# Token rows of expert 4 issued by ScalarE, behind its gate function of expert 2, in place of SyncE

## The reference, cut to what matters

```
scores = sigmoid(x @ w_router)                  # 384 tokens, 16 experts in 4 groups
best group by the sum of its top 2; top 2 experts of that group; weights w normalised
act = silu(x @ w_gate[e]) * (x @ w_up[e])       # w_gate, w_up: 1024 x 512 per expert
y = sum over the two chosen e of w[e] * (act @ w_down[e])   # w_down: 512 x 1024
```

## Time and profile before

| | us |
|---|---|
| median of 3 runs | 1435.25 (1432.86 to 1435.38) |
| the profiled execution | 1432.73 |
| its span, first to last instruction | 1430.9 |
| TensorE busy | 1298.1 (91%) |
| VectorE busy | 496.8 (35%) |
| ScalarE busy | 318.8 (22%) |
| share of q1 (SyncE's queue) of the DMA engines' span | 61.1% |
| share of q10 (ScalarE's queue) | 4.2% |
| mean granted clock of TensorE | 0.979 |

### The profile page before, as it was taken

One profiled execution on the slowest core, in us unless ns is written; L12 is line 12 of the kernel. 1 busy time (PEld: TensorE's weight loads), 2 busy tenths in 40 slices (PEclk: granted clock), 3 DMA queues, 4 the chain that ended last, 5 costly groups with the idle time before them and its releaser, 6 DMA issues.

```text
span 1430.9 us, 17501 instructions
## 1 busy us (share of the span) xinstructions
PE 1298.1 (91%) x6833; PEld 742.8 (52%) x6834; DVE 496.8 (35%) x881; ACT 318.8 (22%) x489; POOL 259.0 (18%) x225
## 2 busy tenths in 40 slices
PE   6999999999999969889879999999999999998773
PEld 3555446675546535445536554555655554554431
DVE  2325427862145101111154353577413531110104
ACT  2136416631001100000021562464100110000001
POOL 2730017821000100000128000684200010000001
PEclk9999999999999979999989999999999999999998
DMA  9897426654437999999974231576442579999996
GB/s 348 259 344 265 177 84 230 220 192 148 176 117 296 355 380 386 387 396 391 415 255 138 69 112 59 175 242 238 163 176 118 216 278 366 367 387 386 408 416 261
DMA packets 117049, 371.85 MB, mean 260 GB/s; under 512 B 18016, under 2 KB 33024, under 8 KB 100336
## 3 DMA queue, kind: packets, MB, share of 16 engines
q1 hardware_dynamic: 86496, 329.69, 61.1%
q0 software_dynamic: 6480, 21.95, 4.2%
q10 hardware_dynamic: 24000, 19.21, 4.2%
HBM read 341.40 MB, written 29.43 MB: 259 GB/s over the span
## 4 chain that ended last, share of the span: by engine, by line
PE 72%; DMA 14%; DVE 8%; issue 2%; ACT 2%; SPq 1%; ACTq 0%; POOL 0%; DVEq 0%
PE pG L1749 24%; PE pS L1838 11%; PE pG L1741 10%; PE pG L1994 6%; PE pG L1856 6%; DMA ring<-in_w_exp_up_dram 6%; DMA modb<-in_w_exp_up_dram 3%; PE pX L1679 3%; PE pX L1838 2%; DMA hT_gen<-x_scr 2%; PE pG L1712 2%; DMA ring<-in_w_mod_dram 2%; PE pS L1780 1%; DVE ring L1326 1%; PE pX L1804 1%
## 5 line engine op out<-in xcount | busy, mean ns | idle before, releaser
L1749 PE MATMUL pG<-hT_gen,ring 128*128 128x384 f32 x1024 | 339.6, 489 | 1.6 <-ACT hT_gen L1061 1.6
L1749 PEld LDWEIGHTS pG<-hT_gen,ring 128*128 128x128 f32 x1024 | 191.8, 190 | 141.5 <-issue 13.7
L1838 PE MATMUL pS<-ring,hT_gen 128*64 128x256 f32 x1344 | 155.9, 388 | 15.7 <-DMA ring<-in_w_exp_up_dram 6.8
L1741 PE MATMUL pG<-ring,hT_gen 128*128 128x512 f32 (+1 forms) x384 | 150.8, 549 | 5.1 <-ACT hT_gen L928 2.9
L1838 PEld LDWEIGHTS pS<-ring,hT_gen 128*64 128x64 f32 x1344 | 104.7, 140 | 69.3 <-issue 14.6
L1614 DVE TENSOR_TENSOR hT_gen<-pS,hT_gen 128x256 f32<-128x256 f32 x32 | 19.2, 601 | 329.6 <-PE pS L1838 329.6
L1741 PEld LDWEIGHTS pG<-ring,hT_gen 128*128 128x128 f32 x384 | 72.3, 192 | 74.8 <-issue 68.3
L820 POOL DMA_INDIRECT ring<-y_scr,idx x12 | 11.4, 946 | 483.7 <-ACTq L1138 480.7
L1856 PE MATMUL pG<-ring,hT_gen 128*64 128x512 f32 x352 | 82.4, 610 | 11.5 <-DVE hT_gen L1617 8.8
L708 POOL TENSOR_TENSOR stat<-stat,half 128x1 f32<-128x1 f32 (+3 forms) x30 | 28.7, 956 | 310.1 <-DVE stat L1279 209.9
L1994 PE MATMUL pG<-ring,hT_gen 128*128 128x512 f32 x192 | 83.1, 592 | 0.0
(11 more groups left out here) (302 smaller groups left out, 1638.8 us busy)
## 6 DMA issues: line engine op xcount, KB each, us to landing
ring<-in_w_mod_dram SPq DMA_DIRECT2D x24, 2048.0 KB, 8.6
ring<-in_w_exp_up_dram SPq DMA_DIRECT2D x22, 2048.0 KB, 25.4
ring<-in_w_in_dram SPq DMA_DIRECT2D x20, 2048.0 KB, 8.8
ring<-in_w_exp_down_dram SPq DMA_DIRECT2D x20, 2048.0 KB, 24.4
ring<-in_w_exp_gate_dram SPq DMA_DIRECT2D x20, 2048.0 KB, 24.6
modb<-in_w_exp_up_dram SPq DMA_DIRECT2D x10, 2048.0 KB, 30.2
hT_gen<-in_w_exp_down_dram SPq DMA_DIRECT2D x10, 2048.0 KB, 29.7
rows_nw<-in_w_exp_gate_dram SPq DMA_DIRECT2D x10, 2048.0 KB, 30.3
```

Source lines behind the costliest of these rows:

```text
L1741: ins = pe.matmul(ps[:, 0:width], hT[:, k, t * P:(t + 1) * P], w[:, k, 0:width], start=(k == 0), stop=(k == KC - 1))
L1749: ins = pe.matmul(ps[:, 0:TOK], w[:, k, c0:c0 + P], src[:, k, :], start=(k == 0), stop=(k == nk - 1))
L1838: ins = pe.matmul(dst[64 * hf:64 * hf + 64, 0:256], x[:, k, :], w[k][:, 256 * hf:256 * (hf + 1)], start=(k == 0), stop=(k == KC - 1))
```

## The change

ScalarE gets a `token_rows` of its own, and issues the two DMAs of the rows of expert 4 in its stream for expert 2, after its Silu and its further blocks, and before it waits for the down product. SyncE no longer issues them: after the gate product of expert 2 (and its further blocks' products) it goes on to the wait for the up product and the up weights of expert 5. The bytes, the buffer, the semaphore and all waits of TensorE stay. It happens once a layer, four DMAs in all.

```diff
@@ SyncE, behind(p, c, ahead)
                     further_done(p * 3 + c, gate_and_up=True)
-                    if c == 2:
-                        token_rows(4, xrow[1], x_got[1])
-                    else:
+                    if c != 2:
                         e, part = follow[0]
                         expert(L, p * 3 + e, slots_of(e)[part], part)
@@ ScalarE
+                def token_rows(row, dst, s):
+                    for hf in range(2):
+                        act.dma_start(dst[BLK * hf:BLK * (hf + 1), :],
+                                      x_scr[row * BLK:(row + 1) * BLK, 512 * hf:512 * (hf + 1)]).then_inc(s, 16)
+
                 def expert_of(p, c, load=True, first=False):
...
                     if first and c == 2:
                         further_blocks(c)
+                        token_rows(4, xrow[1], x_got[1])
                     act.wait_ge(e_down, n + 1)
```

## The result

The changed kernel takes 1438.12 us (median of 13 runs, 1435.02 to 1443.41) where the kernel before takes 1434.5 us (13 runs, 1431.37 to 1438.98). The ratio is 1.0026, with a 95% interval of 1.0014 to 1.0038: slower by 3.7 us, between 2.0 and 5.5.

What follows compares the result with a forecast made beforehand. The weight stream was taken to bound the expert stages, in the second layer from 1217 us on. First layer 0, second -0.4 + 2.2 = +1.8 us, on 1435.25 gives 1437.0 us; range 1432.0 to 1441.0.

Steps and rivals of the forecast that it cites:

- The first layer, 0 us: First layer's experts: wait for expert 4's rows falls from 13.65 to 3.3 us, but the weight stream eats the gain.
- Up 9: First layer, sign: the up weights of expert 9 still land within 1 us of 600.9.
- SyncE's issues, -0.4 us: Second layer: expert 5's up weights go out 1.15 us earlier, less 0.73 us for the rows' transfer competing with weights.
- The new wait, 8.6 us: Second layer, expert 3: rows queued on q10 behind the further store land about 1237.5, while TensorE wants them at 1228.89.
- rival (c): Second layer: longer dip, 4.5 us lost, plus 1 us from low clock in the first; +5.1 us, 1440.3; chance 0.20.
- The dip, 2.2 us: Second layer: expert 3's down-weight slot frees late, stream loses 3.7 us, of which q10 transfers fill 1.5.
- TensorE meets the stream again before the end: Second layer: TensorE, some 10 us late, gains 5 us an expert and meets the stream by expert 12, before 1400.
- The sum: Whole kernel: first layer 0, second layer -0.4 + 2.2, together +1.8 us.
- (a): First layer: the removed wait is a gain of the kernel, 10.3 us less, 1425.0; chance 0.07.
- (b): Second layer: no dip, only the earlier issue counts, 0.4 to 1.15 us gained, 1434.5; chance 0.17.
- (d): First layer: rows on q10 come no earlier than on q1; time as forecast; chance 0.04.

Runs made afterwards that it cites:

- e1: The change in the first layer only, second layer as before, against the kernel before: 1433.37 us against 1433.2, ratio 1.0005.
- e3: Kernel before, but in the first layer expert 4's rows are fetched early into another buffer and copied, removing the wait for rows: 1433.71 us against 1433.2, ratio 1.0007.
- e4: Kernel before, but in the second layer SyncE issues expert 4's rows behind the up weights of expert 5: ratio 1.0000 against before.
- e5: Kernel before, but in the second layer SyncE issues expert 4's rows behind expert 5's up and down weights: ratio 1.0000 against before.
- e6: The changed kernel, but in the second layer ScalarE issues the rows ahead of the further block's store: 1430.83 us against 1433.53 before, ratio 0.9989.
- e9: The changed kernel, but in the second layer TensorE turns expert 4's rows behind expert 3's down product, its first loop turn written out: ratio 1.0026 against before.

## Why the prediction was right, point by point

**The first layer, 0 us: right.** The wait fell to 4.34 us where 3.3 was forecast (the second half of the rows lands 17.9 us after its issue, not 15.7), and the stream ate it, as e1 and e3 show. Up 9 moved by 0.64 us, within the 1 us that was named. In the change run again it moved by 0.8 us the other way. The waits for weights began at expert 7. The stage itself took 1.4 us longer in one profile and 1.0 us less in the other, so no cost is seen. Two details differ: the waits were to begin at expert 6, and the end of the stage was to be set by TensorE's own path, while in one of the two profiles it waited 1.60 us for up 15.

**SyncE's issues, -0.4 us: not seen.** The up weights went out earlier (59.95 us into the stage, before 61.11), as forecast. e4, which has the earlier issue without the new wait, shows 1.0000 (0.9987 to 1.0013); 0.4 us is below what these runs can tell.

**The new wait, 8.6 us: 9.83.** The order on q10 was the one that was read from the earlier trace rows. The second half landed 13.7 us after its issue, where 12.4 us had been counted (and where rival (c) began at 14).

**The dip, 2.2 us: 4.75. This term was mis-sized.** The forecast let the weight stream lose 3.7 us and filled 1.5 of them with four transfers left on q10. The trace of the changed kernel shows both halves off. Landings of the stores of 1228.0 us, of the rows of expert 6 of 1229.3, of up 6 of 1230.69 and of down 6 of 1247.66:

```profile
DMA to landing us min/median/max: 15.1/15.7/16.3
...
DMA to landing us min/median/max: 15.2/15.3/15.3
...
DMA to landing us min/median/max: 14.0/14.0/14.0
...
DMA to landing us min/median/max: 9.5/9.5/9.5
```

Up 6 is in at 1244.7 and down 6 at 1257.2, 12.5 us apart in place of 6: the weights lose 6.5 us, since the stream was done 0.7 us sooner than forecast, the slot came 0.8 us later (both on the scale of before) and the load into the empty queue took 9.5 us, not 8.3. And the stores and rows on q10 were in by 1244.9 and 1245.2 us: they shared the engines up to the same instant as the weights, so they filled nothing of the gap behind it (51 GB/s in the stretch from 1245). The engines' idle time, 4.75 us, is less than the 6.5 us that the weights lost; what they did in the rest isn't separated (ScalarE issues the next stores and rows at 1248.4 and 1249.8, beside down 6). The step that failed, besides the gap and the refill being 1.5 and 1.2 us too short, is the sentence "on q10 lie the two stores and the two rows of expert 6, which get the engines to themselves for that time".

**TensorE meets the stream again before the end: right.** It waits for weights from expert 11's up weights on (2.25 us at 1341.71) until 1406.71. The lateness of some 11 us behind expert 3 costs nothing of itself; e5 shows the same with 3.5 us.

**The sum.** +1.8 us was forecast, 3.7 (2.0 to 5.5) measured. The mechanism and the layer are those of the forecast; the size is not. For the second layer rival (c), with the same place and 4.5 us for it, comes to -0.4 + 4.5 = 4.1 us, which is what the stages show; only its further 1 us in the first layer was not seen. With the dip at its 4.75 us and the rest as it stood, the sum would have been 4.4. That the time forecast, 1437.0, lies only 1.1 us below the 1438.12 measured is in part luck: it was added to a median of three runs, 1435.25, where thirteen gave 1434.5. The difference itself was missed by 1.9 us. Rivals (a) and (b) did not happen, and (d) neither: the rows came some 9 us earlier in the first layer. The rule of the Trainium skill (page "DMA: Bandwidth & Descriptors", section "Issuing engines are not separate DMA queues", that spreading DMAs over engines only saves issue time) held for the stream as a whole, 0 in e1. For one small DMA, of whose delay the rule says nothing, the choice of queue is a choice of what stands ahead of it: 28.1 us on q1, 17.9 us on q10, and 2.8 us on that same q10 where nothing stood there and the engines were quiet (e6).

## What to carry to other kernels

A long wait of the busiest engine is worth nothing while the DMA engines are full and the engine waits for the same stream further on: look for the next wait on that stream, and ask whether the landing would move. What can cost is the other direction, a wait that holds up the release of a buffer until the stream's queue runs dry, and it costs only from that point: 3.5 us of waiting were free here, 9.8 us cost about 4. That it is the held buffer and not the wait as such is what the profiles say and e9 supports. When a small DMA is moved to another queue, look at what is queued ahead of it there and in which spell it is issued, in every layer, since an earlier step of the new issuer (here the store of a further block) can place it 8 us later than before.

## What was not expected of the hardware

- The DMA engines ran dry (share 0.27) not during the 9.8 us in which TensorE stood but in the stretch from 1245 us, 4.5 us behind the end of the wait: weights and small transfers on the two queues ended within 0.5 us of each other.
- Writing out the first turn of a loop on TensorE, with no change of its work, cost 4.0 us (2.0 to 6.0), as much as the whole change, with 58 packets in place of 49 on the instruction queue; a kernel edited for an experiment needs this control.
- Two halves of the same rows, 128 KB each, took from 2.8 us (quiet engines) to 17.9 us (full engines, behind two such transfers) on the same queue.
